# A diffusion trunk's two mixers: decays by doubled products, masks summed before the value product

## The reference, cut to what matters

```python
def step(S, inp):
    qi, ki, vi, gi = inp
    bcum = jnp.cumsum(gi, axis=2)
    b_last = bcum[:, :, -1:, :]
    o_inter = jnp.einsum('bhtd,bhde->bhte', qi * jnp.exp(bcum), S)
    diff = bcum[:, :, :, None, :] - bcum[:, :, None, :, :]
    decay = jnp.where(causal, jnp.exp(jnp.minimum(diff, 0.0)), 0.0)
    att = jnp.einsum('bhtd,bhtsd,bhsd->bhts', qi, decay, ki)
    o = o_inter + jnp.einsum('bhts,bhse->bhte', att, vi)
    S = jnp.exp(b_last[:, :, 0, :])[..., None] * S + jnp.einsum(
        'bhsd,bhse->bhde', ki * jnp.exp(b_last - bcum), vi)
    return S, o
# HGRN2: f = lb + (1 - lb) * sigmoid(f_pre); g = log(max(f, 1e-20)); k = (1 - lb) * sigmoid(-f_pre)
# GLA:   g = log_sigmoid(low @ w_gate + b_gate) / 16; q, k, v = silu(conv(...))
```

## Time and profile before

| | |
|---|---|
| runs, median (lowest to highest) | 4441.62 us (4440.77 to 4447.28), 3 runs |
| profiled execution, span on the chip | 4444.5 us; its time outside the span is not listed |
| TensorE busy over the span | 4093.7 us, 92% |
| VectorE busy | 3686.2 us, 83% |
| ScalarE busy | 1732.4 us, 39% |
| GpSimd busy | 1899.2 us, 43% |
| HGRN heads | from about 140 to 618 us |
| GLA heads | from about 2380 to 2747 us |

### The profile page before, as it was taken

One profiled execution on the slowest core, in us unless ns is written; L12 is line 12 of the kernel. 1 busy time (PEld: TensorE's weight loads), 2 busy tenths in 40 slices (PEclk: granted clock), 3 DMA queues, 4 the chain that ended last, 5 costly groups with the idle time before them and its releaser, 6 DMA issues. The chain is left out here.

```text
span 4444.5 us, 73738 instructions
## 1 busy us (share of the span) xinstructions
PE 4093.7 (92%) x24855; PEld 3709.2 (83%) x24855; DVE 3686.2 (83%) x6798; ACT 1732.4 (39%) x2584; POOL 1899.2 (43%) x1320
## 2 busy tenths in 40 slices
PE   6899988968999999999988997895899999999997
PEld 3899977847899999999977887884799999999997
DVE  6688864998788888999987885498788888999997
ACT  6455533427333333333334443222633333333333
POOL 2100014737545445556552122222644544566664
PEclk9899978989999999999998997897999999999999
DMA  7111123519999999999972112110999999999995
GB/s 288 52 50 55 58 72 119 178 34 225 360 363 363 361 363 355 364 365 360 362 266 59 39 51 74 52 54 9 253 366 361 364 360 363 357 361 363 363 360 222
DMA packets 620190, 1049.51 MB, mean 236 GB/s; under 512 B 229763, under 2 KB 405318, under 8 KB 619590
## 3 DMA queue, kind: packets, MB, share of 16 engines
q1 hardware_dynamic: 471520, 508.69, 34.0%
q0 software_dynamic: 147456, 536.94, 32.3%
q10 hardware_dynamic: 1126, 2.79, 0.2%
HBM read 982.75 MB, written 65.54 MB: 236 GB/s over the span
## 5 line engine op out<-in xcount | busy, mean ns | idle before, releaser
L2083 POOL DMA_INDIRECT rows_ex<-in_peer_v,ctx_index x512 | 703.6, 1374 | 479.7 <-DVE row_acc_ex L2162 364.1
L2083 POOL DMA_INDIRECT rows_ex<-in_peer_u,ctx_index x512 | 586.8, 1146 | 635.4 <-DVE dots_ex L2165 502.4
L2248 PE MATMUL pu_ex<-h_hi,uT_hi_ex 128*128 128x384 f32 x2048 | 715.8, 350 | 1.9 <-ACT coef_ex L2112 1.0
L2162 DVE SCALAR_TENSOR_TENSOR row_acc_ex<-rows_ex,factor_ex,row_acc_ex 128x1024 f32<-128x1024 f32 x512 | 657.7, 1284 | 56.3 <-issue 17.6
L2248 PE MATMUL pu_ex<-h_lo,uT_hi_ex 128*128 128x384 f32 x2048 | 692.8, 338 | 0.0
L2248 PE MATMUL pu_ex<-h_hi,uT_lo_ex 128*128 128x384 f32 x2048 | 692.8, 338 | 0.0
L2256 PE MATMUL py_ex<-v_hi_ex,c_hi_ex 128*128 128x512 f32 x1536 | 622.5, 405 | 0.0
L2165 DVE CUSTOM_DVE_ANT_0 rows_ex<-rows_ex,h_row_ex 128x1024 f32<-128x1024 f32 x512 | 604.2, 1216 | 0.0
L2256 PE MATMUL py_ex<-v_lo_ex,c_hi_ex 128*128 128x512 f32 x1536 | 601.0, 391 | 0.0
L2256 PE MATMUL py_ex<-v_hi_ex,c_lo_ex 128*128 128x512 f32 x1536 | 600.6, 391 | 0.0
L2101 ACT ACTIVATE uT_hi_ex<-pT_ex 128x512 fp32r<-128x512 f32 x512 | 304.0, 594 | 509.4 <-PE pT_ex L2241 486.2
(11 more groups left out here) (446 smaller groups left out, 8422.9 us busy)
## 6 DMA issues: line engine op xcount, KB each, us to landing
u_raw_ex<-in_peer_u SPq DMA_DIRECT2D x256, 512.0 KB
v_raw_ex<-in_peer_v SPq DMA_DIRECT2D x256, 512.0 KB
gates<-stage_ro SPq DMA_DIRECT2D x12, 4096.0 KB, 16.0
g_raw_ex<-gates SPq DMA_DIRECT2D x256, 192.0 KB
ada<-in_ada_w SPq DMA_DIRECT2D x12, 2048.0 KB, 11.8
ada_re<-in_ada_w SPq DMA_DIRECT2D x16, 1536.0 KB, 6.8
w_raw_hgrn<-in_hgrn_w_in SPq DMA_DIRECT2D x40, 512.0 KB
w_raw_re<-in_peer_w_q SPq DMA_DIRECT2D x32, 512.0 KB, 5.7
```

What stands on the lines that cost most here:

```text
L2083: pool.indirect_dma_start(out=rows[m % RING][:, :], out_offset=None, in_=a["peer_u" if m < TG * NC else "peer_v"].rearrange("l n d -> (l n ...
L2162: nc.vector.scalar_tensor_tensor(row_acc[g][:, :], rows[j][:, :], factor[:, j:j + 1], row_acc[g][:, :], ALU.mult, ALU.add).then_inc(row_fr ...
L2248: last_ = nc.tensor.matmul(pu[:, 0:TD], w[:, k, :], x[:, k, 0:TD], start=(k == 0 and w is uT_hi[b] and x is h_hi), stop=(k == DC - 1 and w ...
```

## The change

Per head and direction the program no longer sums logarithms. It keeps `run`, four planes: query and key, forward and backward, with their decays multiplied up within blocks. `run` starts as query x decay (and the bare key) for blocks of one token; seven doubling steps each multiply one half of every pair of blocks by the sibling's total decay (`tots`), in place. The values that `run` has before step s are the factors of one level, so they are copied out into `ex` first: the forward direction by ScalarE (`keep`), the backward direction by GpSimd. After the seventh step `run` holds the factors for the states.

The scores of a head's five tiles are all kept in PSUM (`pS`): coarse levels in one plane per tile, the fine levels and the own score in 32x32 blocks. VectorE masks and sums the fine ones (`fm`, `near`), spreads them into `am` and lays the coarse plane over them with a predicated copy. The output of a tile is then one product with `am` and two with the states. In HGRN the decay's affine map moves from VectorE to ScalarE, and the logarithm and the repair of small numbers go. In GLA two convolutions run in turns, tap by tap, and those of query and key for the next head are done at a head's end.

```diff
         @block.gpsimd
...
             def head(h, final):
-                if POOL_LEVELS:
-                    pool.wait_ge(b_ready, h + 1)
-                for l in range(POOL_LEVELS):
-                    exponents(pool.tensor_tensor, l)
-                    pool.drain().then_inc(pool_diff, 1)
+                if mx.gla:
+                    pool.wait_ge(kd_done, h + 1)
+                for s in range(len(STEPS)):
+                    pool.wait_ge(run_at[1], h * (len(STEPS) + 1) + (s + 1))
+                    alone(pool, pool_passed)
+                    pool.tensor_copy(level_slots(1, s), running(1, STEPS[s])).then_inc(kept[1], 1)
                 if not final:
                     lo(h + 1, 0)
                     lo(h + 1, 1)
...
         @block.scalar
+            def keep(h, s0, s1):
+                for s in range(s0, s1):
+                    act.wait_ge(run_at[0], h * (len(STEPS) + 1) + (s + 1))
+                    act.activation(level_slots(0, s), running(0, STEPS[s]), ACT.Copy).then_inc(kept[0], 1)
...
                 else:
                     copy(v[:, 0, :], 0, h)
                     next_hi(h, 0, final)
-                    chunk_exps(h)
+                    keep(h, 0, 2)
                     output_gates(h, 0, final)
                     act.drain().then_inc(og_done, 1)
-                    level_exps(h, 0, 4)
+                    keep(h, 2, 4)
                     if not final:
                         early(h, 0)
-                    turned_copies(h)
-                    level_exps(h, 4, 7)
+                    keep(h, 4, 7)
                     if not final:
                         early(h, 1)
+                    turned_keys(h)
+                    turned_values(h)
+                    if not final:
                         early(h, 2)
+                        decays(h + 1)
...
         @block.vector
+                def decayed_queries():
+                    for d in range(2):
+                        nc.vector.tensor_mul(run[:, 2 * d, :], q, f2[:, d, :]).then_inc(run_at[d], 1)
+
+                def double(s0, s1):
+                    for s in range(s0, s1):
+                        pairs = tots[s][:, :, :].rearrange("p d (n h) -> p d n h", h=2)
+                        nc.vector.tensor_mul(tots[s + 1][:, :, :], pairs[:, :, :, 0], pairs[:, :, :, 1])
+                        for d in range(2):
+                            dve.wait_ge(kept[d], h * len(STEPS) + (s + 1))
+                            nc.vector.tensor_mul(running(d, STEPS[s]), running(d, STEPS[s]), sibling_totals(d, s)) \
+                                .then_inc(run_at[d], 1)
+                        dve.drain()
...
+                    decayed_queries()
+                    double(0, 3)
                     lo(h, 2, final)
-                    chunk_factors()
+                    double(3, 6)
                     lo(h, 3, final)
-                    level_exponents(POOL_LEVELS + 3, NL)
+                    double(6, 7)
                     lo(h, 4, final)
...
+                dve.wait_ge(att, h + 1)
+                for t0, t1 in ((0, 2), (2, NT)):
+                    fine = pS[:, FINE_AT[t0]:FINE_AT[t1 - 1] + NF * FINE].rearrange("p (t l j) -> p t l j", l=NF, j=FINE)
+                    nc.vector.tensor_mul(fm[:, t0:t1], fine, c["fine_mask"][:, :, :].unsqueeze(1)
+                                         .to_broadcast([P, t1 - t0, NF, FINE]))
+                dve.drain()
+                nc.vector.tensor_reduce(near[:, :, :], fm.rearrange("p t l j -> p t j l"), AX.X, ALU.add)
+                dve.drain()
+                nc.vector.tensor_copy(am[:, :, :].rearrange("p t (b j) -> p t b j", j=FINE),
+                                      near[:, :, :].unsqueeze(2).to_broadcast([P, NT, P // FINE, FINE]))
+                dve.drain()
+                nc.vector.copy_predicated(am[:, :, :].rearrange("p t j -> p (t j)"),
+                                          c["coarse_mask"][:, :, :].rearrange("p t j -> p (t j)").bitcast(U16),
+                                          pS[:, 0:NT * P]).then_inc(masked, 1)
...
         @block.tensor
                 for j in range(L):
                     project(h, j)
                 if not final:
                     project(h, L)
+                    if not mx.gla:
+                        project(h, L + 1)
...
+                def near_scores(t, slot, keys, queries):
+                    at = FINE_AT[t] + slot * FINE
+                    for r in range(0, P, FINE):
+                        tok = slice(t * P + r, t * P + r + FINE)
+                        last = nc.tensor.matmul(pS[r:r + FINE, at:at + FINE], keys[:, tok], queries[:, tok],
+                                                start=True, stop=True)
+                    return last
...
-                        terms = [(tt[:, 10 + t * NV + vv, :], am[t % 2][:, l, :]) for l in range(NM)]
+                        terms = [(tt[:, 10 + t * NV + vv, :], am[:, t, :])]
                         if t < NT - 1:
-                            terms += [(S[:, d, t, vv * P:(vv + 1) * P], e2[:, d, tok]) for d in range(2)]
+                            terms += [(S[:, d, t, vv * P:(vv + 1) * P], run[:, 2 * d, tok]) for d in range(2)]
```

More of the change, by code:

```diff
@@ L814, in turned_copies @@
[L814 to L823 removed]
+                    return
@@ L1154, in head, with turn_values @@
-                if not final:
-                    project(h, L + 1)
+                    for r, src in enumerate(tiles):
+                        last = nc.tensor.transpose(turned_bank(g)[:, r, :], src, c["ident"][:, :])
+                    last.then_inc(turned, 1)
+                def turn_values():
+                    if mx.gla:
+                        pe.wait_ge(v_ready, h + 1)
+                    for i, tiles in enumerate(VALUE_TURNS):
+                        turn(len(KEY_TURNS) + i, [v[:, n % NV, n // NV * P:(n // NV + 1) * P] for n in tiles])
@@ new lines, in head @@
+                for g, (first, tiles) in enumerate(KEY_TURNS):
+                    turn(g, [run[:, 1 + 2 * d, t * P:(t + 1) * P] for _, d, t in tiles])
+                if not mx.gla:
+                    turn_values()
+                for d in range(2):
+                    pe.wait_ge(kept[d], h * len(STEPS) + len(STEPS))
+                if mx.gla:
+                    pe.wait_ge(kd_done, h + 1)
+                for l in range(3):
+                    for t in range(NT):
+                        level_scores(t, l)
@@ L1156, in head @@
+                for l in range(3, NL):
+                    for t in range(NT):
+                        level_scores(t, l)
+                for t in range(NT):
+                    last = near_scores(t, NF - 1, kd, q)
+                last.then_inc(att, 1)
+                if mx.gla:
+                    turn_values()
                 pe.wait_ge(turned_out, h * NG + NG)
-                pe.wait_ge(o_out, h * NT + 1)
                 for i, (d, t) in enumerate(WITH_STATE):
@@ L1181, in own_scores @@
-                def own_scores(t):
-                    tok = slice(t * P, (t + 1) * P)
-                    nc.tensor.matmul(pA[t % 2][:, NM - 1, :], kd[:, tok], q[:, tok], start=True, stop=True) \
-                        .then_inc(att, 1)
-                def scores(t):
-                    pe.wait_ge(masked, h * NT + (1 + t - 1))
-                    for l in range(NL):
-                        level_scores(t, l)
-                    own_scores(t)
-                pe.wait_ge(masked, h * NT + 1)
```

441 lines of the change are left out of this document (188 added, 253 removed).

## The result

The changed kernel takes **4459.2 us** (median of 5 runs, 4456.7 to 4462.9) beside 4441.5 us for the kernel before on the same chip: ratio 1.0039, 95% interval 1.0027 to 1.0051, so 17.7 us slower. I had forecast 4481 us: slower, as it came, but by 39.5 us. The profiled execution has a span of 4458.4 us, its own time is 4460.1. I read it in the order in which the prediction was made.

What follows compares the result with a forecast made beforehand. HGRN was taken as bound by TensorE with VectorE close behind, GLA by both in turns. HGRN +48 and GLA -9 us made +39 on the 4444.5 us span, less 2.9: 4481 us, range 4436 to 4530.

Steps and rivals of the forecast that it cites:

- the circle: HGRN head: VectorE's weight splits wait through doublings and ScalarE's copies on TensorE's last projection; TensorE idles 5.3 and 8.0 us.
- the slow stretches: HGRN projections behind the two waits: TensorE at 1.2 GHz after idling, 2.1 us each, 4.2 us a head.
- the wait for GpSimd's split of chunk 0: HGRN head: GpSimd's split, 2.4 us long, ends after the now short outputs; 0.9 us.
- The second circle: HGRN head, behind projection 2: two doubling steps (5 and 6 of 7) before the next split; TensorE waits 8.0 us.
- The failed step: Scores per head: 40 small records at 0.017 us replace ten larger ones per tile, 0.7 for 1.2 us; 2.6 us off.
- dear end: Small score records at 0.036 us each, not 0.017; gives 3.8 us per head back.
- The outputs' term: HGRN head: one masked product in place of six per tile, 10 records x 0.112 x 5 tiles; 5.6 us off.
- The 12.7: GLA head: TensorE's wait after projection 3 for the values' convolution and what follows, 21.8 us against 8 us of work.
- the scores' term: GLA head: smaller score blocks take 2.6 us off, within 13.8 us of TensorE work removed.
- GpSimd's lock: Rival 1: GpSimd's copies hold VectorE at every split, 3.1 us per HGRN head, giving 4513 us; chance 0.18.
- no slow clock: Rival 2: idle stretches of 5 us leave TensorE's clock alone, giving 4439 us, no change; chance 0.11.
- GLA gains more than HGRN loses: Rival 3: values' convolution ends before TensorE's transposes, GLA heads take 80 us, giving 4416 us; chance 0.09.

Runs made afterwards that it cites:

- Experiments 1 to 3: Edits of the changed kernel's HGRN heads: both splits earlier, 4348.2 us; only chunk 2's split earlier, 4403.7; unread filler matmuls in TensorE's waits, 4452.3, with fewer 4434.5.
- experiment 3: Changed kernel with unread filler matmuls ahead of HGRN projections 2 and 3: 60 and 90 gave 4452.3 us, 40 and 60 gave 4434.5 us.
- experiment 5: Changed kernel with HGRN splits earlier, GLA's transposed keys copied first and values' convolution between doublings: 4294.0 us; with GLA filler matmuls added, 4290.8 us.
- experiment 7: Changed kernel, fine score blocks: same rows in succession, 4496.1 us; each group issued twice, 4510.6; an unread full matmul behind each group, 4611.3.
- the run with the same rows: Changed kernel with the block of rows in the outer loop, so 25 fine score blocks in succession go to the same 32 rows: 4496.1 us.

## Why the prediction was right, and where it was wrong

**The bound and the direction.** Right: the circle that I read out of the order binds. The two waits on L1002 came at 5.45 and 7.45 us, forecast 5.3 and 8.0; the slow stretches at 4.2 us, as forecast; the wait for GpSimd's split of chunk 0 at 1.08, forecast 0.9. Experiments 1 to 3 show by removal that the circles and the slow clock are what they were called; nothing tested the wait for chunk 0. The second circle is shorter than forecast because I had GpSimd's copy and two products one after the other, 2.8 us: they took 2.1 (315.89 to 318.02), the copy beside the first product. And my 1.1 for this copy met the mean of 1.16 by luck: it is the mean of copies of 0.72 us and of copies that waited.

**The failed step** is the term "2.6 us per head" for the shrunken scores. Measured in an HGRN head it is 5.5: a tile took 1.79 us from its first score to its first output (258.54 to 260.33 in the trace before) and takes 3.48 / 5 = 0.70. The earlier trace rows gave 0.0165 for blocks that stand before a full product, and the earlier trace rows 0.036 beside them, while the change puts all small blocks one behind the other and they take 0.009. I had kept a dear end for this price and no cheap one. That is 1.7 of the 2.9 us; the other 1.2 are the coarse blocks, whose 0.58 us per tile I had left as it was and which came to 0.34 (80 records in 1.7 us). The outputs' term was near: 9.1 us before (4 x 1.88 and 1.6), 3.07 after, 6.0 off for 5.6. Against this, the transposes cost 0.9 more than before, for 0.4. An inner head came to +6.8 for +9.1, of which these measured terms leave some 0.6 us open; six such heads are 14 us of the 22 that my sum was too high.

**First and last HGRN head.** The last was -8.2 for -8. The first was +3.8 for +1: I had not counted 3.9 us in which TensorE stops in the new score code for nothing that the profile shows, where it runs for the first time. The DMA view has 3 packets of the instruction queue between 194 and 206 us, where these stops lie, and none from there to 606 us, in which no head has such stops: they go together with the loading of instructions.

**GLA** gained 18 for 9. The waits were near the forecast: 13.7 for 12.7 at the transposes, 4.7 (6.3 in the next head) for 6.4, 1.0 for the split's 1.5, 2.8 for 2.6 in small pieces, in sum 22.2 for 23.2. The 12.7 was a slip: its own terms, 21.8 less 8 of work, give 13.8, which is what was measured. TensorE's busy time was 66.6 for 69.9 (65.7 and 4.2 of slow clock); the scores' term, 2.9 us too small at full clock, is most of that. So the inner heads were -3.4 and -2.9 for 0. The first head was -4.7 for +3, the last -7.3 for -12: opposite misses of 8 and 5 us that I can't put down to single rows.

**The rivals.** 1, GpSimd's lock: the engines do exclude each other, but at the splits VectorE comes first, and only some 0.5 us of the forecast 3.1 per head is there. 2, no slow clock: refuted by experiment 3. 3, GLA gains more than HGRN loses: did not happen, since the values' convolution did stand where I said; with it moved (experiment 5) the GLA head even fell to 76.3, below the 80 of that rival.

**What I did not ask** was how far the new waits were a matter of order. I priced the change as written; 165 us, nine times what it costs, lay in the places of five splits, half a convolution and two groups of copies, and my own description of the circle named them.

## What to carry to other kernels

When work that a consumer waits for (here VectorE's weight splits, for TensorE) stands in program order behind a step that waits for a third engine's copy, which in turn stands behind the consumer's last work, the circle costs its whole length at each turn: here 13 us of idle TensorE in a head in which no engine was busy for more than 78% of the time. Look for the producer's earliest free place before pricing anything else. Take the price of a small matmul only from rows with the same neighbours. A change that removes work from the engine that bounds should be tried with its waits reordered before it is judged: as made it cost 0.4%, reordered it gains 3.3%.

## What the runs showed of the hardware that I had not expected

- TensorE's 32-column blocks cost 0.009, 0.030 or 0.043 us a record by what stands beside them, all at a granted clock of 1.00 (experiment 7).
- GpSimd's copy of 640 elements took 0.72 us where it came first and 1.80 where it started together with a split on VectorE, which kept its 1.23; a product beside the first kind of copy took 1.36 for 0.82.
- The granted clock fell to 0.50, the level of 1.2 GHz, in a stretch in which the profile calls TensorE busy throughout (9.00 of 9.00 us, small blocks and full products in turn), and 18 us behind the end of its last long wait (7.45 us). The 6 us of small blocks of the run with the same rows kept 1.00.
- A filler product of 128 columns took 0.11 us (6.81 / 60), twice what I had put for it.
- 200 more small matmul records in a GLA head brought stops without a releaser, 6.5 and 5.9 us in its repeated heads, and 17 instruction packets in these two heads, where the change has none.
